# First expert block: its rows are picked for three token tiles ahead of the last tile's positions

## The reference

```python
logits = x2d @ router_w + router_b                # 512 x 32
top_val, top_idx = lax.top_k(logits, TOP_K)       # 4 of 32 experts a token
gate = jax.nn.softmax(top_val, axis=-1)
...                                               # assignments sorted by expert, in blocks of rows
hg, hl = jnp.split(xblk @ w_gu[e] + b_gu[e], 2, axis=-1)
glu = hg * jax.nn.sigmoid(hg * SWIGLU_ALPHA)      # with clamps on hg and hl
y = ((hl + 1.0) * glu) @ w_down[e] + b_down[e]    # weighed by gate and added to its token
```

## Time and profile before

| | |
|---|---|
| median of 3 runs | 3219.87 us (3217.14 to 3225.6) |
| the profiled execution, its own time | 3227.16 us |
| span of the profiled execution | 3225.3 us |
| PE busy | 3063.4 us (95%) |
| DVE, ACT, POOL busy | 1121.9, 539.1, 152.6 us |
| TensorE clock granted, mean | 0.973 of full speed |
| moved to and from HBM | 674.98 MB read, 67.13 MB written |

### The profile page before, as it was taken

One profiled execution on the slowest core, in us unless ns is written; L12 is line 12 of the kernel. 1 busy time (PEld: TensorE's weight loads), 2 busy tenths in 40 slices (PEclk: granted clock), 3 DMA queues, 4 the chain that ended last, 5 costly groups with the idle time before them and its releaser, 6 DMA issues.

```text
span 3225.3 us, 52638 instructions
## 1 busy us (share of the span) xinstructions
PE 3063.4 (95%) x22479; PEld 1721.5 (53%) x22479; DVE 1121.9 (35%) x2273; ACT 539.1 (17%) x1132; POOL 152.6 (5%) x91
## 2 busy tenths in 40 slices
PE   9888988899999999999999999999999999999999
PEld 3365545343333334333345667755677648766776
DVE  1634453222323222232364432453134241354222
ACT  1333210111111111111112220120103100031000
POOL 0000002000000000000020000001011000011110
PEclk9898888899999999999989999999999999999999
DMA  9900046899999999999862323423433343343442
GB/s 400 361 1 27 27 174 244 324 403 402 407 400 405 403 405 404 404 401 406 353 259 105 138 108 131 157 88 141 157 144 141 137 173 148 131 151 133 167 157 104
DMA packets 97467, 743.70 MB, mean 231 GB/s; under 512 B 11128, under 2 KB 38336, under 8 KB 57552
## 3 DMA queue, kind: packets, MB, share of 16 engines
q1 hardware_dynamic: 58768, 687.49, 54.1%
q10 hardware_dynamic: 32624, 30.52, 3.0%
q0 software_dynamic: 5968, 24.14, 2.0%
HBM read 674.98 MB, written 67.13 MB: 230 GB/s over the span
## 4 chain that ended last, share of the span: by engine, by line
PE 54%; DMA 29%; DVE 4%; issue 2%; ACT 2%; ACTq 1%; POOL 1%; DVEq 0%
DMA arena<-x_sorted 28%; PE psum L1882 19%; PE psum L1754 8%; PE psum L1706 5%; PE psum L1849 3%; PE psum L1717 3%; PE psum L982 2%; ACTq L713 1%; PE psum L964 1%; PE psum L1521 1%; PE psum L1485 1%; PE psum L1362 1%; PE psum L1577 1%; DMA x_sorted<-arena 1%; PE psum L1623 1%
## 5 line engine op out<-in xcount | busy, mean ns | idle before, releaser
L1410 PE MATMUL psum<-weight_ring,arena 128*32 128x512 f32 x6192 | 677.3, 594 | 48.3 <-DVE arena L3243 47.5
L1882 PE MATMUL psum<-arena,weight_ring 128*128 128x256 f32 (+1 forms) x2816 | 630.2, 383 | 3.1 <-ACT arena L2543 3.1
L1882 PEld LDWEIGHTS psum<-arena,weight_ring 128*128 128x128 f32 x2816 | 528.3, 189 | 95.7 <-issue 7.1
L1410 PEld LDWEIGHTS psum<-weight_ring,arena 128*32 128x32 f32 x6192 | 199.5, 110 | 506.4 <-issue 460.8
L1485 PE MATMUL psum<-weight_ring,arena 128*32 128x256 f32 x6144 | 338.2, 380 | 0.0
L1485 PEld LDWEIGHTS psum<-weight_ring,arena 128*32 128x32 f32 x6144 | 196.7, 110 | 152.9 <-issue 26.8
L3265 DVE STREAM_TRANSPOSE arena<-arena 128x384 f32<-128x384 f32 x32 | 18.6, 580 | 662.8 <-DMA arena<-x_sorted 662.8
L3671 DVE TENSOR_TENSOR weight_ring<-weight_ring,psum 128x256 f32<-128x256 f32 (+1 forms) x88 | 37.4, 425 | 472.1 <-PE psum L1882 471.5
L1706 PE MATMUL psum<-weight_ring,arena 128*128 128x512 f32 (+2 forms) x512 | 170.0, 489 | 3.1 <-ACT arena L2543 3.1
L980 PE MATMUL psum<-arena,weight_ring 128*128 128x512 f32 x288 | 135.9, 625 | 10.5 <-DMA weight_ring<-weights 6.2
L1706 PEld LDWEIGHTS psum<-weight_ring,arena 128*128 128x128 f32 x512 | 96.0, 190 | 70.5 <-issue 59.8
(11 more groups left out here) (468 smaller groups left out, 2938.6 us busy)
## 6 DMA issues: line engine op xcount, KB each, us to landing
weight_ring<-exp_gu SPq DMA_DIRECT2D x129, 2048.0 KB, 11.8
weight_ring<-weights SPq DMA_DIRECT2D x104, 2048.0 KB, 7.8
weight_ring<-exp_down SPq DMA_DIRECT2D x64, 2048.0 KB, 11.3
x_sorted<-arena SPq DMA_DIRECT2D x2, 10752.0 KB
arena<-x_sorted ACTq DMA_DIRECT2D x132, 96.0 KB, 19.8
y_sorted<-arena ACTq DMA_DIRECT2D x128, 96.0 KB, 17.0
y_sorted<-arena SPq DMA_DIRECT2D x2, 5632.0 KB, 39.4
y_sorted<-arena SPq DMA_DIRECT2D x2, 5120.0 KB, 37.8
```

The source lines that it names most:

```text
L1410: mm = pe.matmul(psum[j * GROUP:(j + 1) * GROUP, g, :], xg[:, k // 4, g, k % 4 * GROUP:(k % 4 + 1) * GROUP], w[:, kk, j * 512:(j + 1) * 51 ...
L1882: mm = pe.matmul(bank[:, 0:b - a], w[:, k, col:col + P], h2_t[:, k, a:b], start=(k == 0), stop=(k == KT - 1))
```

## The change

- `PICK_BANK` becomes (0, 1): the picked rows go into two banks of `v_ring` that are free by then, in place of banks 6 and 7.
- On PE, `place(bank, 2)` now signals `places_begun`. Behind it PE waits for `first_rows_ready` (first count), and picks the rows of tiles 0, 1 and 2 for both halves: 24 of the 32 matmuls. Only then stands `place(bank, 3)`, and the bank is shipped. The last tile's 8 matmuls stay in `experts`.
- On DVE, between `choose(2)` and `choose(3)`, a wait for `places_begun` and `first_places` for tiles 0 to 2: the two instructions that form `first_rows`, three quarters of them, read straight from the bank in PSUM. In `route` the same two are left for tile 3 alone.
- `gate_up(0)` of the first block now writes into the banks that hold the picked rows, so its second group waits for the second copy by ACT (`rows_turned` 2).

```diff
-        PICK_BANK = (6, 7)
+        PICK_BANK = (0, 1)
+        PICK_JOBS = 2 * TT - 1
...
-                place(bank, 2)
+                place(bank, 2).then_inc(sem("places_begun"), 1)
+                pe.wait_ge(v_ring.drained, PICK_JOBS)
+                pe.wait_ge(sem("x1_by_tile_ready"), TT - 1)
+                pe.wait_ge(sem("first_rows_ready"), 1)
+                for half in range(2):
+                    pick_rows(half, range(TT - 1))
                 v_ring.ship(place(bank, 3))
+
+            def pick_rows(half, tiles):
+                for k in range(4):
+                    for t in tiles:
+                        at = (4 * half + k) * P
+                        mm = pe.matmul(psum[:, PICK_BANK[half], k * ROWS_B:(k + 1) * ROWS_B], y[:, t, at:at + P],
+                                       first_rows[:, t, :], start=(k == 0 and t == 0), stop=(t == TT - 1), skip_group_check=True)
+                return mm
...
-                pe.wait_ge(sem("first_rows_ready"), 1)
+                pe.wait_ge(sem("first_rows_ready"), 2)
                 pe.wait_ge(sem("x1_by_tile_ready"), TT)
                 for half in range(2):
-                    pick_rows(half).then_inc(sem("rows_picked"), 1)
+                    pick_rows(half, (TT - 1,)).then_inc(sem("rows_picked"), 1)
...
                 def first_used(g, mm):
+                    if mm is None and g == PICK_BANK[1]:
+                        pe.wait_ge(rows_turned, 2)
...
-                for t in (1, 2, 3):
+                for t in (1, 2):
                     choose(t)
+                dve.wait_ge(sem("places_begun"), 1)
+                first_places(slice(0, TT - 1), v_ring.psum[:, v_ring.at(v_ring.taken), 0:TT * E].rearrange("p (t e) -> p t e", t=TT))
+                choose(TT - 1)
+
+            def first_places(tiles, places):
+
+                n = tiles.stop - tiles.start
+                iota = CONST3(c3, "iota")[:, 0:ROWS_B].rearrange("p (o r) -> p o r", o=1).broadcast_to([P, n, ROWS_B])
+                first = first_at.rearrange("p (t o) -> p t o", o=1)[:, tiles]
+                then(dve.scalar_tensor_tensor(first, assigned[:, tiles, 0:1], -1024.0, places[:, tiles, 0:1], ALU.mult, ALU.add))
+                then(dve.scalar_tensor_tensor(first_rows[:, tiles, :], iota, -1024.0, first.broadcast_to([P, n, ROWS_B]), ALU.add, ALU.is_equal),
+                     sem("first_rows_ready"))
...
-                first = first_at.rearrange("p (t o) -> p t o", o=1)
-                then(dve.scalar_tensor_tensor(first, assigned[:, :, 0:1], -1024.0, pos[:, :, 0:1], ALU.mult, ALU.add))
-                then(dve.scalar_tensor_tensor(first_rows, iota[:, 0:ROWS_B].rearrange("p (o r) -> p o r", o=1).broadcast_to([P, TT, ROWS_B]),
-                                              -1024.0, first.broadcast_to([P, TT, ROWS_B]), ALU.add, ALU.is_equal), sem("first_rows_ready"))
-
+                first_places(slice(TT - 1, TT), pos)
```

## The result

| | median us | runs |
|---|---|---|
| before | 3220.11 (3210.51 to 3232.89) | 13 |
| after | 3235.84 (3230.83 to 3240.03) | 13 |

The ratio is 1.0047, with a 95% interval of 1.0035 to 1.0059: the change costs 15.1 us, between 11.3 and 19.0. That is slower by more than 0.3%. The forecast, 3228.0, had the sign and about half of the size.

A forecast was written before the change was run, and what follows sets the result against it. Taken as the bound: the full DMA stretch before the second block, whose beginning `dest` on DVE sets. The copy 8.45 us later, less 0.30, gave +8.15 us, all passed on: 3228.0 us against the median 3219.87; range 3219 to 3237.

The forecast's parts named there:

- the 48 pick matmuls: PE ahead of `place(3)`: 32 at the low clock and 16 at the high one, 9.0 us, bounds 5.5 and 10.7.
- the copy: DVE's copy of the counts after `place(3)`: starts at 526.1 and not at 517.65, 8.45 us later.
- the shorter pair behind it: DVE's two instructions behind the copy: 384 to 96 columns, 0.56 to about 0.26 us, a gain of 0.30.
- the rival of the sooner clock: PE's picks: clock rises sooner, picks take 7.5 or 5.5 us, +6.65 or +4.65 us, 3224.5 to 3226.5; chance 0.14.
- the first block: PE in `experts`: picks end 0.9 us sooner, worth nothing because PE then waits for the biases.
- an absorbed delay: Loop behind the second block's start: the later start is caught up, no change, 3219.9 us; chance 0.08.
- filled gaps: PE is the bound and picks fill its gaps: 0.9 us sooner at the first block passed on, 3219.0; chance 0.04.
- the step to the median: Whole kernel: +8.15 us on the profiled 3227.16 gives 3235.3; against the median of 3219.87, forecast 3228.0 us.
- the range: Whole kernel's time: from the absorbed case, 3219, to the low clock with its hole and some spread, 3237.
- a low clock that lasts, with a hole in the DMA stretch: PE's picks and `place(3)` all slow: +10.3 us, 3230.2; with a hole in the DMA stretch +12.3, 3232.2; chance 0.17.
- the DMA term: DMA engines before the second block: idle stretch grows by 8.15 us, full stretch keeps its bytes and ends 8.15 later.
- The clock's spread: PE's picks: by the skill's rule the clock's rise differs between runs, making the term a spread from 7.5 to 10.7 us.

The follow-up runs named there:

- e4: The kernel before, unchanged, run again for a second profile: 3215.56 us in one run.
- e8: Kernel before, with SP asking for the second block's first weights only when that block's rows have landed: 3218.57 us, ratio 1.0001.
- e1: Kernel before, with the product in front of `dest` repeated 11 times more, so `dest` comes 7.9 us later: 3234.54 us, ratio 1.0064.
- e6: Changed kernel, with SP asking for the second block's first weights only when the scatter has landed: 3232.06 us, ratio 1.0037.
- e11: Changed kernel, with the 24 early picks put behind `place(3)` instead of in front of it: 3226.72 us, ratio 1.0025.
- e9: Changed kernel, with SP asking for the second block's first weights only when that block's rows have landed: 3225.15 us, ratio 1.0030.
- e12: Changed kernel, with early picks behind `place(3)` and SP's weights waiting for the second block's rows: 3218.60 us, ratio 1.0000, without one run of 3294.93.
- e2: Kernel before, with the picks in banks 0 and 1 and the second wait for `rows_turned`: 3217.17 us, ratio 1.0000.
- e7: Kernel before, with the product in front of `dest` repeated 23 times more, `dest` about 16 us later: 3246.28 us, ratio 1.0078.

## Why the prediction was half right

- **Right, PE and DVE.** `first_places` took 0.16 and 0.46 us (forecast 0.19 and 0.46), the 48 pick matmuls 8.51 (9.0), the copy came 7.83 later (8.45), the shorter pair behind it is 0.16 + 0.26. The clock rose about 6.2 us after the picks' start, not 7.2 (0.94 granted from 523.90 to 526.40 is a step at about 524.2). That is the whole difference, and the rival of the sooner clock is right by so much.
- **Right, the first block.** `gate_up(0)` came 1.28 us sooner (0.9), PE waited 9.13 us for the biases (9), and neither bought any time.
- **Right against its own execution.** The second block was 7.04 us later than in the first profile, against 8.15 forecast. The rivals of an absorbed delay and of filled gaps fall between these two: the loop gave nothing back beyond noise (second block's matmul to the loop's end 1041.55 us after, 1042.42 before; the loop ends at 1626.92 and 1619.17). Against e4 and e8 a part was given back, as said under the table.
- **Wrong, the step to the median.** "against the median the forecast is 3228.0 us": I took the 7.29 us between the profiled execution and the median for noise that both kernels share. By e4 it was the collision itself, though two profiles of before are few. In the usual execution of before there is no wait in front of the second block (e4), and the change brings one of 18.10 us. So the cost against the usual kind is the change's own 7 us plus what the collision costs: 20.9 us at the second matrix against e4, 15.1 in the whole time by the ratio.
- **Luck, the range.** The result lies inside 3219 to 3237, but the upper part of that range stood there for a low clock that lasts, with a hole in the DMA stretch. The clock did not last, it rose sooner; what filled the upper part was the collision, which no rival named. The chance of a result slower by more than 0.3% was put at 0.34.
- **Wrong, the DMA term.** "the bytes of the full stretch stay the same ... so its end moves by the same 8.15 us". The second block does not wait for the bytes but for those of the scatter and the rows among them. With the weights beside them (after, e1, e6, e11) or mostly behind them (e4, e9, e12) the same bytes end at other times; e9 and e12 show it with one wait on SP.
- **The clock's spread.** The prediction quoted the Trainium skill (TensorE: Matmul & The Clock Gate, Part 1) that the moment of the rise differs from run to run. The traces agree: the same 64 pick matmuls took 10.79 us in the first profile of before, 10.74 in e4 and 9.19 in e2. It did not set the size of the error.

Shown: the delay alone is enough (e1), the banks cost nothing (e2), the cost is a step and then about the delay itself (e1, e7), and ordering the weights behind the rows takes 8 us off e11. Off the changed kernel it takes some 5 (ratios 1.0047 and 1.0030, whose intervals overlap; the profile has the second block 12 us sooner). Of the changed kernel's cost 9.7 us (6.1 to 13.5) remain with that order; that they are the late `dest` passed on is argued from e9's wait for weights which SP could not ask for earlier. Not settled: what holds PE and SP while the scatter fills the engines, and so why `gate_up(0)` of the kernel before is sometimes stretched and sometimes not.

## What to carry to other kernels

Before a profile is subtracted from a median, look at a second profile of the same kernel: where runs differ by 10 us, the one at hand may have a wait that the usual run has not. Where one queue's landing gates the next stage, ask which other transfers an earlier or later engine will put beside it; order them by a wait on the issuing queue, and don't count only the bytes. Work that depends on nothing late does not belong in front of the last small step of a chain that everything waits for.

## What was not expected of the hardware

- With the DMA engines full of the scatter's packets, PE stood in pieces of 0.8 to 1.8 us between matmuls in front of which the profile shows no wait, and 48 matmuls that take 5.36 us took 17 (531.34 to 548.30, e4). SP too: in e11 its waits from 528 to 590 us (us in total, times, longest) name no instruction of this program for 13.8 us, in which piece 0 could have been asked for:

```profile
SPq L2036 <- remote: 13.8, 1, 13.8
```

What these are stays open. The traces list loads of instructions as DMA queues of their own (q8, q14), but from 524 to 552.9 us neither e4 nor e11 has a packet of them; the next stand at 554.0 and 553.0, when the gaps are over. So no such load ended a gap.

- A load of 393 KB was used 3.8 us after its issue with the engines free, 9.7 us with one piece of weights 2.9 us ahead and one 4.7 us behind (e4), 19.5 and 23.3 us with four beside it (e6, e11).
